# A two-block transformer kernel: order of the FFN-up matmuls, of the first group's copies and of the latent transposes, and a bias table in one pass

## The reference

```python
# first block
h = rmsnorm(x, attn_norm_w)
rq, rk, rv, rg, mq, mk, mv, g_ret, g_moba = split(h @ w_in)
merged = sigmoid(g_ret) * (o_ret @ w_ret_up) + sigmoid(g_moba) * (o_moba @ w_moba_up)
x = x + merged @ w_out
up = causal_dwconv(rmsnorm(x, ffn_norm_w) @ w_ffn_up, conv_w, conv_b)   # 2048 x 11264, width 3
a, b = split(up)
x = x + (silu(a) * b) @ w_ffn_down                                       # 5632 x 2048
x = rmsnorm(x, final_norm_w)
# second block: three attention branches from one projection of rms_norm(x)
#  A: 8 heads; keys chosen by an index score (top 64 of 256), with
bias = rel_table[t5_bucket(pos_q - pos_k)]                               # 32 buckets x 8 heads
logits = where(valid, q @ k * scale + bias, -inf)
#  B: queries and keys from normed latents of 512 and 256 columns
qb = rms_norm(bcq, g) @ w_b_uq;  kv = rms_norm(bckv, g) @ w_b_ukv
#  C: attention over a memory of 256 tokens
merged = sum over branches of sigmoid(gate) * ((o * silu(z)) @ w_branch)
x = x + merged @ w_out
```

## Time and profile before

| | us |
|---|---|
| median of 3 runs | 2490.83 (2490.19 to 2491.08) |
| the profiled execution | 2490.3 |
| its span on the core | 2488.5 |
| TensorE matmul busy | 2476.3 |
| VectorE busy | 1498.8 |
| ScalarE busy | 1237.0 |
| GpSimd busy | 235.7 |
| mean granted TensorE clock | 0.999 of full speed |

### The profile page before, as it was taken

The page is one execution under the profiler, slowest core; times in us unless marked ns, Lnnn a source line. Parts: engine busy times, 40 slices in busy tenths (PEclk is TensorE's granted clock), DMA queues, the critical chain, the costliest instruction groups (busy, mean ns, idle before and its releaser), DMA issues.

```text
span 2488.5 us, 36014 instructions
## 1 busy us (share of the span) xinstructions
PE 2476.3 (100%) x11895; PEld 2055.3 (83%) x11895; DVE 1498.8 (60%) x1798; ACT 1237.0 (50%) x1655; POOL 235.7 (9%) x277
## 2 busy tenths in 40 slices
PE   8999999999999999999999999999999999999999
PEld 7888888878888888888888888888887788877887
DVE  4445445577656777777777776444457555554564
ACT  5445455555445444444444445454547556555443
POOL 0011224231000000000000000010101000432000
PEclk9999999999999999999999999999999999999999
DMA  7655555566655555555555556654564545444654
GB/s 247 194 185 170 169 174 174 175 213 205 209 187 177 187 186 192 185 187 189 189 185 188 188 189 211 201 185 170 171 210 162 170 164 182 163 157 144 228 185 162
DMA packets 131139, 461.08 MB, mean 185 GB/s; under 512 B 14465, under 2 KB 17793, under 8 KB 130433
## 3 DMA queue, kind: packets, MB, share of 16 engines
q1 hardware_dynamic: 122336, 443.60, 53.6%
q10 hardware_dynamic: 8736, 16.58, 2.0%
HBM read 454.36 MB, written 5.77 MB: 185 GB/s over the span
## 4 chain that ended last, share of the span: by engine, by line
PE 97%; DVE 1%; ACT 1%; DMA 0%; issue 0%; POOL 0%; ACTq 0%; POOLq 0%; DVEq 0%; SPq 0%
PE PS L607 21%; PE PS L609 20%; PE PS L608 20%; PE PS L842 13%; PE PS L844 7%; PE PS L866 3%; PE PS L868 3%; PE PS L867 3%; PE PS L689 1%; PE PS L706 1%; PE PS L669 1%; PE PS L648 1%; DVE WL L1466 1%; ACT WH L991 1%; PE PS L781 0%; PE PS L697 0%
## 5 line engine op out<-in xcount | busy, mean ns | idle before, releaser
L1466 DVE TENSOR_TENSOR WL<-RAW,WH 128x1024 fp32r<-128x1024 f32 x842 | 1054.4, 1255 | 934.7 <-ACT WH L991 929.8
L991 ACT ACTIVATE WH<-RAW 128x1024 fp32r<-128x1024 f32 x842 | 890.5, 1060 | 1139.0 <-PE PS L609 746.3
L607 PE MATMUL PS<-WH,HT 128*128 128x512 f32 (+1 forms) x1816 | 725.4, 399 | 5.6 <-DVE HT L1495 3.6
L609 PE MATMUL PS<-WH,HT 128*128 128x512 f32 (+1 forms) x1816 | 708.8, 390 | 0.0
L608 PE MATMUL PS<-WL,HT 128*128 128x512 f32 (+1 forms) x1816 | 707.1, 389 | 0.0
L842 PE MATMUL PS<-HT,WH 128*128 128x512 f32 x1408 | 498.2, 399 | 0.0
L607 PEld LDWEIGHTS PS<-WH,HT 128*128 128x128 f32 x1816 | 341.8, 188 | 78.8 <-issue 8.9
L609 PEld LDWEIGHTS PS<-WH,HT 128*128 128x128 f32 x1816 | 341.2, 188 | 72.0
L608 PEld LDWEIGHTS PS<-WL,HT 128*128 128x128 f32 x1816 | 342.2, 188 | 66.0
L844 PE MATMUL PS<-HT,WL 128*128 128x256 f32 x1408 | 395.8, 281 | 0.0
L842 PEld LDWEIGHTS PS<-HT,WH 128*128 128x128 f32 x1408 | 264.8, 188 | 65.4
(11 more groups left out here) (259 smaller groups left out, 1938.5 us busy)
## 6 DMA issues: line engine op xcount, KB each, us to landing
RAW<-w_stream SPq DMA_DIRECT2D x842, 512.0 KB, 3.3
X<-x_in SPq DMA_DIRECT2D x4, 512.0 KB, 7.4
MEMR<-mem_in ACTq DMA_DIRECT2D x1, 2048.0 KB, 11.5
X<-x_in ACTq DMA_DIRECT2D x4, 512.0 KB, 4.1
x_scratch<-X ACTq DMA_DIRECT2D x4, 512.0 KB, 5.5
X<-x_scratch ACTq DMA_DIRECT2D x1, 2048.0 KB, 8.3
out<-X ACTq DMA_DIRECT2D x8, 256.0 KB, 3.1
bias_scratch<-BE ACTq DMA_DIRECT2D x12, 128.0 KB, 2.5
```

The costliest lines, as they stand in the source:

```text
L607: pe.matmul(o, hi, WH[:, slot, kk, 0:cols], start=k == 0, stop=False)
L609: ins = pe.matmul(o, lo, WH[:, slot, kk, 0:cols], start=False, stop=k == nq * GK - 1)
L991: act.activation(WH[:, g.slot(j)], RAW[:, g.slot(j)], ACT.Copy).then_inc(hi_split, 1)
L1466: dve.tensor_tensor(WL[:, s], RAW[:, s], WH[:, s].bitcast(F32), ALU.subtract).then_inc(lo_split, 1)
```

## The change

- TensorE, FFN up: within each half group (one `kk`) the four wide matmuls come first, then the four narrow ones. The counts are the same. In the phase's very first group this is done in twos.
- First group: ScalarE and VectorE do the tiles of step q right after the splits up to `SPLIT_FIRST[q]`, so tiles 4, 5 follow split 2, tiles 6, 7 split 3, tiles 8, 9 splits 4 and 5, and so on.
- ScalarE's queue loads PARAM before CONST.
- Latent transposes and their halves move from steps 4 to 6 to steps 3 to 5; the mask adds from steps 3, 4 to 5, 6; GpSimd no longer waits for `sel_ready` (TensorE's scores are used by VectorE, which still does).
- Bias: both parts of REL are the 64 stationary columns of one matmul, 2 per step in place of 4; the copy and the stores cover 64 partitions. High and low parts are loaded into BIAS and BIASL by eight DMAs in the odd steps 1 to 15 of the phase `c_proj` and added there by VectorE in steps 26 and 28. The loop of ScalarE and VectorE over that phase is written out.

```diff
         BIAS = sb("BIAS", [P, REL_HEADS, CAUS], F32, at_u2)
+        BIASL = sb("BIASL", [P, REL_HEADS, CAUS], F32, at_u1)
         LATT = sb("LATT", [P, 6, 2, S], F32R, at_sgx + 4 * KB)
...
         OH = sb("OH", [P, 2, 8, P], F32R, at_x + 4 * KB)
-        BE = sb("BE", [32, 8, P], F32, at_x + 12 * KB)
+        BE = sb("BE", [64, 8, P], F32, at_x + 12 * KB)
         RAW = sb("RAW", [P, RING, GK, CH], F32, take(16 * KB))
...
         PS = ctx.enter_context(nc.psum_tensor("PS", [P, 8, 512], F32))
-        bias_scratch = nc.dram_tensor("bias_scratch", (32, 3, 32, P), F32, kind="Internal").ap()
+        bias_scratch = nc.dram_tensor("bias_scratch", (64, 3, 32, P), F32, kind="Internal").ap()
         x_scratch = nc.dram_tensor("x_scratch", (S, D), F32, kind="Internal").ap()
...
         BIAS_AT = (2, 4, 7, 10, 12, 15)
+        SPLIT_FIRST = (1, 2, 3, 5, 6, 7, 8, 11)
         def pairs_ahead(q):
...
             inverse_roots(MST[:, 1, :, 0:2])
-            hold(sel_ready, 2)
             with pool.Fori(0, 2) as kv:
...
                 for b in range(2):
-                    for part in range(2):
-                        ins = pe.matmul(PS[0:32, 4 + b, :], REL[:, part, :],
-                                        OH[:, k.base % 2, 4 * b:4 * b + 4, :].rearrange("p q s -> p (q s)"), start=part == 0, stop=part == 1)
+                    ins = pe.matmul(PS[0:64, 4 + b, :], REL[:].rearrange("p a n -> p (a n)"),
+                                    OH[:, k.base % 2, 4 * b:4 * b + 4, :].rearrange("p q s -> p (q s)"), start=True, stop=True)
                 ins.then_inc(bias_done, 1)
...
                 half = 4 * (u.base % 2)
-                in_turn = [(kk, f) for kk in range(GK) for f in range(FT)]
-                far_first = [(kk, f) for fs in ((2, 3), (0, 1)) for kk in range(GK) for f in fs]
                 pe.wait_ge(ffn_free, u.count(1))
...
                         late = q == 0 and products_before is not None
-                        for kk, f in far_first if late else in_turn:
-                            k = q * GK + kk
-                            if late and (kk, f) == (0, 0):
+                        for fs in ((2, 3), (0, 1)) if late else (range(FT),):
+                            if late and 0 in fs:
                                 pe.wait_ge(prod_free, 2 + products_before)
-                            pe.matmul(PS[:, half + f, :], WH[:, slot, kk, f * P:(f + 1) * P], HT[:, k, :, :],
-                                      start=k == 0, stop=False, skip_group_check=True)
-                            ins = pe.matmul(PS[:, half + f, 0:S], WL[:, slot, kk, f * P:(f + 1) * P], HT[:, k, 0, :],
-                                            start=False, stop=k == KT - 1, skip_group_check=True)
+                            for kk in range(GK):
+                                k = q * GK + kk
+                                for f in fs:
+                                    pe.matmul(PS[:, half + f, :], WH[:, slot, kk, f * P:(f + 1) * P], HT[:, k, :, :],
+                                              start=k == 0, stop=False, skip_group_check=True)
+                                for f in fs:
+                                    ins = pe.matmul(PS[:, half + f, 0:S], WL[:, slot, kk, f * P:(f + 1) * P], HT[:, k, 0, :],
+                                                    start=False, stop=k == KT - 1, skip_group_check=True)
                         return ins
...
             def latent_tiles(_, p):
-                if 4 <= p < 7:
+                if 3 <= p < 6:
                     pe.wait_ge(lat_rows, 1)
-                    transposes("lat", PB, [2 * p - 8, 2 * p - 7])
+                    transposes("lat", PB, [2 * p - 6, 2 * p - 5])
             def a_step(i, p):
...
                                      lambda: head_probs(br, H), lambda: head_output(br, H, h))))
+            act.dma_start(PARAM[:, 0:KT], params[:, 0:KT]).then_inc(attn_loaded, 16)
             act.dma_start(CONST[:, 0:NFIRST], constants[:, 0:NFIRST]).then_inc(con_loaded, 16)
-            act.dma_start(PARAM[:, 0:KT], params[:, 0:KT]).then_inc(attn_loaded, 16)
             act.sem_inc(prod_free, 2)
...
             transposed("h1", HT, pairs_ahead(0)[2:], "attn")
-            for j in range(1, RING):
-                split(At(0), j)
+            split(At(0), 1)
+            for q in range(1, GD):
+                for j in range(SPLIT_FIRST[q - 1] + 1, SPLIT_FIRST[q] + 1):
+                    split(At(0), j)
+                transposed("h1", HT, pairs_ahead(q), "attn")
             g = At(GROUP0["moba_proj"])
-            for p in range(2 * GD):
-                if 0 < p < GD:
-                    transposed("h1", HT, pairs_ahead(p), "attn")
-                split(g, p + RING)
+            for p in range(GD - 1, 2 * GD):
+                if p >= GD:
+                    split(g, p + RING)
                 if p == GD - 1:
...
                 act.wait_ge(bias_stored, k.count(1) * 16)
-                act.activation(BE[:].rearrange("p (b q) s -> p b (q s)", b=2), PS[0:32, 4:6, :], ACT.Copy).then_inc(bias_copied, 1)
+                act.activation(BE[:].rearrange("p (b q) s -> p b (q s)", b=2), PS[0:64, 4:6, :], ACT.Copy).then_inc(bias_copied, 1)
                 act.wait_ge(bias_copied, k.count(2))
...
             act.wait_ge(x_stored, 16 * NCH)
-            project("c_proj", 2, lambda c: PB[:, :, ds(c, CH)])
+            for p in range(4 * GD):
+                g = At(GROUP0["c_proj"])
+                split(g, p + RING)
+                evacuations("c_proj", g, 0, p, 4, lambda c: PB[:, :, c:c + CH])
+                if p % 2 and p < 4 * RING:
+                    part, r = p // 8, 32 * (p // 2 % 4)
+                    h = 32 * part + 8 * (p // 2 % 4)
+                    act.dma_start((BIASL if part else BIAS)[r:r + 32].rearrange("p h (s k) -> p h s k", s=3),
+                                  bias_scratch[h:h + 8].rearrange("h s p k -> p h s k")).then_inc(bias_loaded, 16)
             act.wait_ge(prod_free, 2 + PROD0["a_proj"])
...
             act.wait_ge(head_out, C0 + 4 + 1)
-            act.wait_ge(bias_stored, 16 * (NBIAS + 1))
-            for g in range(4):
-                act.dma_start(BIAS[32 * g:32 * g + 32, :, :].rearrange("p h (s k) -> p h s k", s=3),
-                              bias_scratch[8 * g:8 * g + 8].rearrange("h s p k -> p h s k")).then_inc(bias_loaded, 16)
             squares = [(PAC[:, h // 4, t, h % 4 * P:(h % 4 + 1) * P], MST[:, 0, t, h:h + 1]) for h in range(8) for t in range(T)]
...
                     act.activation(PB[:, :, PB_Z:PB_Z + W], PB[:, :, PB_Z:PB_Z + W], ACT.Silu).then_inc(gate_ready, 1)
-                elif 4 <= p < 7:
-                    transposed("lat", LATT, [2 * p - 8, 2 * p - 7], "lat")
+                elif 3 <= p < 6:
+                    transposed("lat", LATT, [2 * p - 6, 2 * p - 5], "lat")
             gates_b("gates_b0", 0, 1, latent_steps)
...
             transposed("h1", HT, pairs_ahead(0)[2:], "attn")
-            for j in range(1, RING):
-                split(At(0), j)
-            for p in range(2 * GD):
-                if 0 < p < GD:
-                    transposed("h1", HT, pairs_ahead(p), "attn")
+            split(At(0), 1)
+            for q in range(1, GD):
+                for j in range(SPLIT_FIRST[q - 1] + 1, SPLIT_FIRST[q] + 1):
+                    split(At(0), j)
+                transposed("h1", HT, pairs_ahead(q), "attn")
+            for p in range(GD, 2 * GD):
                 split(At(GROUP0["moba_proj"]), p + RING)
...
                 transposed("h3", HT, h3_tiles(p), "norm2")
-            stream("c_proj", 2, 2 * GD)
+            for p in range(4 * GD):
+                split(At(GROUP0["c_proj"]), p + RING)
+                if p in (26, 28):
+                    dve.wait_ge(bias_loaded, 128)
+                    half = slice((p - 26) * 2, (p - 26) * 2 + 4)
+                    dve.tensor_tensor(BIAS[:, half], BIAS[:, half], BIASL[:, half], ALU.add)
             dve.wait_ge(gate_ready, 2)
...
                                                   op0=ALU.mult, op1=ALU.add))
-                if 4 <= p < 7:
-                    transposed("lat", LATT, [2 * p - 8, 2 * p - 7], "lat")
-                if p in (3, 4):
-                    dve.wait_ge(bias_loaded, 64)
-                    half = BIAS[:, (p - 3) * 4:(p - 2) * 4]
+                if 3 <= p < 6:
+                    transposed("lat", LATT, [2 * p - 6, 2 * p - 5], "lat")
+                if p in (5, 6):
+                    half = BIAS[:, (p - 5) * 4:(p - 4) * 4]
                     dve.tensor_tensor(half, half, SC[:, 0:CAUS].unsqueeze(1).broadcast_to([P, REL_HEADS // 2, CAUS]),
```

## The result

| | before | after |
|---|---|---|
| median of 4 runs, us | 2490.88 (2490.19 to 2491.08) | 2475.82 (2475.48 to 2476.68) |
| the profiled execution, its span | 2490.3, 2488.5 | 2476.06, 2474.2 |
| TensorE matmul busy | 2476.3 | 2466.3 |
| mean granted TensorE clock | 0.999 | 1.000 |

The ratio is 0.9941 [0.9928, 0.9954]: 15.1 us faster, 1.9 us short of the 17.0 of the sum.

What follows compares the result with a forecast made beforehand. TensorE's matmuls were taken to bound the kernel, busy 2476.3 of 2488.5 us. Gains 5.5 + 5.6 + 1.4 + 4.5 = 17.0 gave 2473.3 from 2490.3, 2473.8 on the median's scale; range 2465 to 2482.

Steps and rivals of the forecast that it cites:

- Part 1: Start: tiles copied ahead of late splits, group 2's product begins near 15.6; gain 5.5 us, bounds 3.5 to 6.0.
- I take 0 for them: Start: params loaded first gain 0, since group 2's weights, at 12.34, set the end of this piece.
- rival (d): Start only half mended: TensorE still pauses, clock still falls; 2 us of Part 1 lost, 2477 to 2482; chance 0.08.
- Part 2: Bias in one pass: two matmuls fewer in each of 12 steps; gain 5.6 us, bounds 5.3 to 5.7.
- the rule with which I began: TensorE bounds the kernel: only fewer or denser matmuls, or the end of a stall, pay.
- Part 3: Latent transposes one step sooner, BIAS adds two steps later: TensorE's wait goes; gain 1.4 us, bounds 0.7 to 1.4.
- Part 4: FFN up, four wide then four narrow: denser pitch, 1.400 against 1.413 per four pairs; gain 4.5 us.
- behind four shorts: FFN up: four wide matmuls at 0.930, as behind four short transposes; four pairs 1.382, gain 10.8 us.
- all settled, 1.360: FFN up's upper bound: every matmul at its settled pitch, four pairs 1.360, gain 18.6 us.
- Rival (a): FFN up: order changes nothing, each narrow matmul is too short for the next weight load; 2478.3; chance 0.27.
- Rival (b): FFN up: equal runs settle faster, wide ones at 0.930 or better; 2467.5, to 2460 if all settle; chance 0.2.
- Rival (c): FFN up slower: the 0.188 load shows in full in narrow runs; 2553; decides from pitch about 0.129; chance 0.05.

Runs made afterwards that it cites:

- the run with the old order: Changed kernel with CONST loaded ahead of PARAM and the old order of the first group (splits 1 to 4 ahead of tiles 4 and 5): 2480.58 us.
- the pairs run: Changed kernel with FFN up again in alternating pairs, one wide matmul then one narrow: 2479.35 us, a stretch of 45.21 us.
- the run with 384 columns: Changed kernel with FFN up's narrow matmuls streaming 384 data columns in place of 256, full weights: 2552.72 us, a stretch of 51.86 us.

## Why the prediction was right

**2473.8 was forecast, 2475.8 came,** well inside the range. The 2 us have a place, and one term that came close did so partly by chance.

- **Part 1 (5.5; came 4.4).** The step on the copies was right in mechanism and size: 5.56 by the run with the old order, group 2's product at 15.57 with the constants first. The step that failed is "I take 0 for them", the params. I had said that the constants would come that much later and priced it at one issue, 0.5, without asking who waits for them. The first transposes do. The issue did move by 0.5, but the 96 KB transfer also took 1.6 longer to land (5.9 against 4.3); what X doesn't hide of that is 1.4 at the transposes and 0.6 at group 2's product. The slow pace behind that idle made the rest of its 1.4. The reason given for the 0 failed too: group 2's weights came at 12.33 as before, but they no longer set the end of the piece. Group 1's product on TensorE itself did, which began at 13.78 and not at 12.36. From 16 us on the clock held, so rival (d) did not come as told, though a loss of over half its size did.
- **Part 2 (5.6; came 4.1).** Two matmuls fewer in each of 12 steps is worth 5.78 us once nothing is late, a little above the bound of 5.7. What I left out is the other side of the rule with which I began: a faster TensorE asks for its inputs sooner. I checked what is behind the bias matmuls (copy, stores, loads, adds: all hidden, c projection 87.04 both times) and not what is ahead of them. Before, the one-hot rows ended 0.24 to 0.94 us ahead of their use; a step is 0.47 shorter now, and in five steps nothing of this was left. The rows that would have told were in the trace.
- **Part 3 (1.4; came 1.42).** Right. The tiles' move alone gives 0.64 of it, as VectorE's adds still stand between; how much the adds' move alone gives is not shown.
- **Part 4 (4.5; came 3.9).** The stretch is 44.88 against 44.8. By terms: four wide ones take 0.929 and not 0.948; four narrow ones 0.474 and not 0.452. The first error I had bounded (0.930, "behind four shorts"); the second I had bounded and then taken as nothing in the sum. They nearly cancel, which is luck. In long runs a narrow one behind a narrow one is 0.120 each time, which is the "up to 0.120" that I took for a stall: it is its settled pitch. The 0.113 that I took for settled is the first one behind wide ones. So "all settled, 1.360" and its 18.6 us were out of reach: four pairs at the settled pitches are 1.387, a gain of 9.2 us.
- **Rival (a)** had two halves. "The order changes nothing" is refuted by the pairs run. Of "what is lost belongs to each narrow matmul" half is borne out: 6.6 of its 13 ns a pair are there in every order. The cause that it names, too little time for the load, is not: the same 13.3 ns stand on matmuls of 400 and 512 columns. Yet the load's length does count: with 64 columns of weights the narrow ones take 0.116 on average, not 0.118.
- **Rival (b)** priced the fours at 0.930 for the wide ones, and that came (0.929). Its 10.8 us did not, as it took 0.113 for the narrow ones.
- **Rival (c)** needed a narrow pitch over 0.129; it is 0.118 on average.

The Trainium skill, in TensorE: Matmul & The Clock Gate, section LDWEIGHTS (loading the stationary operand), gives a formula from which 107 ns is the estimate for 128 columns and 53 for 64. By it a narrow matmul of 0.113 just covers its load, and one of 384 columns covers it by far. The recorded loads agree with its slope, 0.188 for 128 columns and 0.134 for 64, 54 ns apart, and not with its level. And by it nothing should depend on the load's length in these runs, while 64 columns in place of 128 saved 4.1 ns a pair.

## What to carry to other kernels

When an edit frees the bounding engine, list what it will ask for sooner and read in the trace by how much each of these inputs is early today; inputs that were 0.4 to 0.9 us ahead here were on the path after the edit. When two issues on a queue are swapped, find who waits first for the one that moves back, above all at a start where nothing is behind which it could hide. And price a change of order by alternating, short and long runs of the real instructions, because each matmul's pitch depends on the shapes of several ahead of it. What an order can gain is measured from the settled pitch of each shape in a run of its own, not from the widest one's scaled down.

## What was not expected of the hardware

**Wide matmuls are slow for several behind narrow ones.** In runs of eight and sixteen, the first wide one behind a narrow one comes after 0.120, the next pitches are on average 233.3, 235.8, 228.3, 232.5 and 230.8 ns, and only then 226.7: 27 ns more than settled. The first two narrow ones behind wide ones give 7.5 of this back (0.113 and 0.119). So a change there and back costs 20 ns in runs of eight and sixteen, 16 in fours, where it is cut short, and 6.6 when each pair alternates.

**A start can run at half pace behind a short idle.** With the params first, TensorE idles 1.5 to 1.8 us ahead of its first transposes, and in 5 of 9 such profiles what follows takes near double: four warm-up matmuls of the changed kernel 1.99 us, against 1.17 to 1.19 in the other four and in all five profiles with the constants first. The first product comes at 10.5 to 10.8 and not at 9.8. The length of the idle doesn't tell the five from the four. In the run with 384 columns the clock's record shows it, at 0.50, the 1.2 GHz level:

```profile
8.20:9.20 1.00, 1.00 (x5) 0.95 (x4) 0.71 (x2) 1.00 (x3) 0.00 (x0) 0.50 1.00 399
```

In the other four of these five the record reads 1.00 at the same slow pace, so that it is the clock there too is likely, not shown.

**VectorE's split stands still while GpSimd works.** A split lasts 1.23 us; one that begins while GpSimd computes distances (L515) ends 1.08 behind it, each of the 12 times. The changed kernel's VectorE, then its GpSimd:

```profile
532.77 1.23 DVE L1474 TENSOR_TENSOR WL<-RAW,WH 128x1024 fp32r<-128x1024 f32 x1 [0.23 <-DVE OH L1655]
534.77 2.06 DVE L1474 TENSOR_TENSOR WL<-RAW,WH 128x1024 fp32r<-128x1024 f32 x1 [0.78 <-ACT WH L993]
...
532.86 2.89 POOL L515 TENSOR_TENSOR DI<-POSB 128x1024 int32<-128x1024 int32 x1 [4.93 <-DVEq L1658]
```

GpSimd ends at 535.75, the second split at 536.83. The Trainium skill says so in SBUF — State Buffer, section Who interferes with whom: a VectorE instruction with two inputs in SBUF and a GpSimd one that reads it take turns, and the second waits for the whole of the first. This trace agrees, both ways round: GpSimd's instruction takes 1.90 where no split runs as it begins (at 487.71) and 2.89 where one had begun 0.09 before it.

This bears on the bias steps. Two splits in a row take 4.06 us so, and the next one-hot rows begin only behind them, in four of the five steps where TensorE waits for the rows:

```profile
542.56 4.06 DVE L1474 TENSOR_TENSOR WL<-RAW,WH 128x1024 fp32r<-128x1024 f32 x2 [0.23 <-DVE OH L1655]
546.54 0.74 DVE L1654 TENSOR_SCALAR OH<-DI,CONST 128x1024 fp32r<-128x1024 int32 x1
```

Distances computed at another time might have made these rows early enough; no run tried it.
